# Prompt attention: the causal mask of the diagonal block, added to the decay rows by GpSimd and taken back by VectorE, in place of bf16 products on TensorE

## The reference

```
s = jnp.einsum('bqhd,bkhd->bhqk', q_blk, k) * (FOX_HD ** -0.5)
s = s + (cq_blk[..., :, None] - ckT[..., None, :])      # cumulated log forget values of query and key
s = jnp.where(kpos[None, :] <= qpos[:, None], s, -jnp.inf)
p = jax.nn.softmax(s, axis=-1)
o = jnp.einsum('bhqk,bkhd->bqhd', p, v)
```

## Time and profile before

| | us |
|---|---|
| median of 3 runs | 1659.86 |
| lowest and highest run | 1656.78, 1660.15 |
| the profiled execution | 1657.8 |
| its span | 1656.2 |

### The profile page before, as it was taken

The page is one execution under the profiler, slowest core; times in us unless marked ns, Lnnn a source line. Parts: engine busy times, 40 slices in busy tenths (PEclk is TensorE's granted clock), DMA queues, the critical chain, the costliest instruction groups (busy, mean ns, idle before and its releaser), DMA issues. The chain is left out here.

```text
span 1656.2 us, 25654 instructions
## 1 busy us (share of the span) xinstructions
PE 1545.4 (93%) x9795; PEld 1401.9 (85%) x9795; DVE 848.9 (51%) x1434; ACT 663.0 (40%) x1117; POOL 241.2 (15%) x297
## 2 busy tenths in 40 slices
PE   7999999999999998999999999999996699999980
PEld 6999899889988887888999999999785588888860
DVE  4433463454035555532232223324657799999985
ACT  5422141212145555521121112113112588888866
POOL 1000111013001211140000000000000345243320
PEclk9999999999999999999999999999997799999995
DMA  6111132124221112073262114103533799999746
GB/s 188 42 39 39 55 117 67 39 67 146 69 81 45 72 46 81 20 236 110 84 198 63 39 39 146 44 34 117 178 115 123 264 260 269 333 301 283 188 64 235
DMA packets 154226, 204.35 MB, mean 123 GB/s; under 512 B 14723, under 2 KB 121235, under 8 KB 154104
## 3 DMA queue, kind: packets, MB, share of 16 engines
q1 hardware_dynamic: 135224, 140.82, 27.2%
q0 software_dynamic: 18880, 61.89, 13.4%
HBM read 152.34 MB, written 50.34 MB: 122 GB/s over the span
## 5 line engine op out<-in xcount | busy, mean ns | idle before, releaser
L380 PE MATMUL ps<-xh,slab_hi 128*128 128x384 f32 (+1 forms) x504 | 170.5, 338 | 1.4 <-DVE slab_lo L733 1.4
L380 PE MATMUL ps<-xh,slab_lo 128*128 128x384 f32 (+1 forms) x504 | 165.2, 328 | 0.0
L380 PE MATMUL ps<-xl,slab_hi 128*128 128x384 f32 (+1 forms) x504 | 164.8, 327 | 0.0
L1906 PE MATMUL ps<-xh,slab_lo 128*128 128x384 f32 (+1 forms) x384 | 125.2, 326 | 0.0
L1906 PE MATMUL ps<-xh,slab_hi 128*128 128x384 f32 (+1 forms) x384 | 125.1, 326 | 0.0
L1906 PE MATMUL ps<-xl,slab_hi 128*128 128x384 f32 (+1 forms) x384 | 125.1, 326 | 0.0
L2122 DVE TENSOR_TENSOR gt_sg<-ps,gt_sg 128x384 f32<-128x384 f32 (+1 forms) x48 | 25.7, 536 | 187.3 <-PE ps L1906 187.2
L380 PEld LDWEIGHTS ps<-xh,slab_hi 128*128 128x128 f32 x504 | 95.1, 189 | 11.5 <-issue 9.7
L2898 PE MATMUL ps<-mo_hi_gu,mo_xh 128*128 128x512 f32 x256 | 100.3, 397 | 0.9 <-ACT mo_xh L3001 0.7
L2062 ACT ACTIVATE gt_sg<-ps 128x384 f32<-128x384 f32 (+1 forms) x48 | 22.8, 474 | 191.9 <-PE ps L1906 191.8
L2898 PE MATMUL ps<-mo_hi_gu,mo_xl 128*128 128x512 f32 x256 | 99.4, 393 | 0.0
(11 more groups left out here) (501 smaller groups left out, 4123.3 us busy)
## 6 DMA issues: line engine op xcount, KB each, us to landing
slab_raw<-in_w_in SPq DMA_DIRECT2D x60, 512.0 KB, 4.2
mo_raw_g<-in_w_e_gate SPq DMA_DIRECT2D x16, 1024.0 KB
mo_raw_u<-in_w_e_up SPq DMA_DIRECT2D x16, 1024.0 KB
mo_raw_d<-in_w_e_down SPq DMA_DIRECT2D x16, 1024.0 KB
gt_oh<-oT_hi SPq DMA_DIRECT2D x3, 2176.0 KB, 9.3
gt_ol<-oT_lo SPq DMA_DIRECT2D x3, 2176.0 KB, 14.0
slab_raw<-in_w_branch SPq DMA_DIRECT2D x24, 256.0 KB, 4.7
x_dram<-slab_raw SPq DMA_DIRECT2D x9, 512.0 KB, 5.1
```

Source lines behind the costliest of these rows:

```text
L380: mm = eng.matmul(out, w[:, b, k, :], x[:, k, t0:t0 + tn], start=(k == 0 and j == 0), stop=(k == KC - 1 and j == 2), skip_group_check=True)
L1906: last = eng.matmul(out, w[:, s % 2, c, wk, :], x[:, k, t0:t0 + tn], start=(k == 0 and i == 0), stop=(k == ks[-1] and i == 2))
```

## The change

The bf16 products go, and with them `mpos`, `ident16` and TensorE's wait for them. A buffer `plain` of three places is new. For block Q, GpSimd's `mask_block(Q)` first copies the decay rows of the block's own 128 keys, for both heads, to `plain`, then adds the mask tile `mf` to them in place. It does this three blocks ahead: for Q = 0, 1, 2 before the loop, and for Q + 3 at the head of its loop step Q. It waits for the rows' load where a pair begins, and for `lowest` of block Q - 2, head 0, before it uses a place of `plain` again. VectorE, before `lowest(Q, 0)`, copies the plain values of block Q - 1 back (not where a pair begins, since those rows aren't read again before they are loaded anew), waits for its own copy, and waits for GpSimd's count, so that the mask of block Q is there.

```diff
-    RW, RH = 2, 4
+    RW, RH, RC = 2, 4, 3
...
-        mpos, ident16 = sb("mpos", [128, 128], BF16), sb("ident16", [128, 128], BF16)
-        mf = sb("mf", [128, 128])
+        mf, plain = sb("mf", [128, 128]), sb("plain", [128, RC, 2, 128])
...
+        def own_block(Q):
+            p, qt = divmod(Q, 8)
+            return cb[:, 2 * (p % 2):2 * (p % 2) + 2, 128 * qt:128 * qt + 128]
...
+            def mask_block(Q):
+                if Q % 8 == 0:
+                    eng.wait_ge(c_in[Q // 8 % 2], 32 * (Q // 16 + 1))
+                if Q >= RC:
+                    eng.wait_ge(s_out, out_no[Q - RC + 1, 0, 0] + 1)
+                ch(eng.tensor_copy(plain[:, Q % RC, :, :], own_block(Q)))
+                ch(eng.tensor_tensor(own_block(Q), own_block(Q), mf[:, :].unsqueeze(1).broadcast_to([128, 2, 128]), ALU.add))
...
-            ch(eng.tensor_copy(mpos[:, :], mf[:, :]))
-            ch(eng.tensor_copy(ident16[:, :], sh.ident[:, :]))
             rows(0)
             rows(1)
+            for Q in range(RC):
+                mask_block(Q)
...
             for Q in range(NQ):
                 p, qt = divmod(Q, 8)
+                if Q + RC < NQ:
+                    mask_block(Q + RC)
                 eng.wait_ge(oT_lo, Q + 1)
...
-                    diag = k0 + n == 128 * (qt + 1)
...
-                                            start=(j == 0), stop=(j == 2 and not diag), skip_group_check=True)
-                    if diag:
-                        for h in range(2):
-                            mm = eng.matmul(sh.ps[:, s_bank(Q, h, c), n - 128:n], ident16[:, :], mpos[:, :], start=False,
-                                            stop=True, skip_group_check=True)
+                                            start=(j == 0), stop=(j == 2), skip_group_check=True)
...
-            eng.wait_ge(pool_s, 4)
             scores(0)
...
+                if h == 0:
+                    if Q % 8:
+                        ch(eng.tensor_copy(own_block(Q - 1), plain[:, (Q - 1) % RC, :, :]))
+                    eng.wait_ge(pool_s, 2 + 2 * (Q + 1))
                 for c in range(n_chunk(Q)):
```

## The result

| | us |
|---|---|
| before, median of 8 runs beside the changed kernel | 1660.01 (1656.78 to 1664.94) |
| after, median of 8 runs | 1666.58 (1664.71 to 1669.67) |
| ratio after to before, 95% interval | 1.0043 (1.0031 to 1.0055) |
| the profiled execution of after, its span | 1667.2, 1665.6 |

The account below looks back on a forecast made before the run. TensorE was taken to set the pace, with VectorE delays counting only where chains through ScalarE end in TensorE's waits. Products -1.5, copies +3.0, collisions +3.2 gave +4.7 us: 1662.5 profiled, 1664.5 as median forecast, range 1657.5 to 1669.5.

Parts of the forecast that it names:

- The gain of the products: TensorE's 64 bf16 mask products go: 0.07 us per block, kept in 22 of 32 blocks, 1.5 us gained (0 to 4.4).
- the nine places: Blocks Q = 3, 5, 7, 11, 13, 15, 19, 21, 28, where VectorE's delay reaches TensorE's wait through ScalarE; no product gain kept.
- block 24's: Block where TensorE waits for a long tail of VectorE, so the removed products were forecast to gain nothing.
- The uncovered copies: VectorE's copies before `lowest` without idle time to cover them: nine blocks by 0.33 us, 3.0 us lost (1.5 to 4.1).
- Rival (b): VectorE's copies never reach TensorE, which keeps all its gain: 2.2 to 6.4 us, 1653.5 to 1657.7 us; chance 0.12.
- The collisions: GpSimd's copy and add hold VectorE's tails and normalisations on the uncovered chains: sum 3.4, taken as 3.2 us (0 to 5.6).
- the row, 0.04 us lost of 0.18 in common: Trace before: VectorE `tensor_tensor` of 128x16 took 0.21 us, not 0.17, beside GpSimd's 128x128 select; read as a small hold.
- rival (e): Every VectorE-GpSimd overlap is paid in full and the add takes 0.78 us: +7.1 us, 1667.0 us; chance 0.07.
- Rival (a): No collisions, GpSimd's copy and add run freely beside VectorE: +1.5 us, 1661.4 us; chance 0.36.
- Rival (c): GpSimd's copy and add slip 20 us, so VectorE waits for late masks: 1671 us or more; chance 0.04.
- Rival (d): The change doesn't do what it says: products stay or other bf16 rows replace them; 1660 us, chance 0.01.

Follow-up runs that it names:

- experiment 2: Changed kernel with VectorE's copies only, bringing back zeros written once, GpSimd's copy and add left out; measured +1.7 us (+0.2 to +3.2) against the kernel before.
- experiment 3: Changed kernel with GpSimd's copy and add kept and VectorE's 28 copies left out; measured +2.0 us (+0.5 to +3.5) against the kernel before.
- experiment 4: Changed kernel with VectorE's copy moved from the head of `lowest(Q, 0)` to behind `out_tail` of the step before; measured +2.8 us (+1.3 to +4.5) against the kernel before.
- Experiment 8: The changed kernel measured again, nothing altered, on the same chip as the other follow-up kernels; +5.6 us (+3.5 to +8.0) against the kernel before, span 1662.5 us.

## Why the prediction was right

**The gain of the products** (forecast 1.5 us from 22 blocks at 0.07). TensorE in order of time behind the scores of block 9, the step of the earlier trace rows, after:

```profile
539.08 0.44 PE L1216 MATMUL ps<-xh,slab_hi 128*128 128x384 f32 x1
539.36 0.34 PE L1216 MATMUL ps<-xl,slab_hi 128*128 128x384 f32 x1
```

0.28 us, the very number of the earlier trace rows. Without a mask, the steps outside the nine places and block 24's are shorter by 1.43 us together, 0.07 each; the nine add 0.26, which the prediction put at nothing. What decided was to price the products by the step that stays when they are gone. By their records, 64 of 0.22 us, one would have expected 14 us.

**The uncovered copies** (forecast 9 x 0.33 = 3.0). Measured 2.9, in the nine places and nowhere else. Reading each chain backwards, from TensorE's wait through ScalarE's queue to a VectorE without idle time before `lowest`, found all nine. Rival (b), that the copies never arrive, falls by experiment 2.

**The collisions** (forecast 3.2, from a sum of 3.4, rounded down without a reason; experiment 3: 3.5). The sum is right by luck: its terms are not, and two errors cancel. The prediction gave 0.2 us to the places Q = 5, 13 and 21; those lost 0.47 to 0.53. In the other direction it charged 0.5 at Q = 11, 15 and 19, which lost 0.26 to 0.28. Two of its inputs were off. It took GpSimd's add at 0.60 us; it takes 0.73. (The 0.7 us that it names as an estimate was near, though not the plain eighth of the 4497 ns beside it, which is 0.56.) And it placed the pair too early. GpSimd's stores begin 0.30 us behind the end of `out_tail` in the kernel before, but in nearly all steps 0.54 behind it in every kernel here that has the pair or the memsets in GpSimd's loop. At Q = 13, before and after:

```profile
558.59 0.29 DVE L1507 TENSOR_TENSOR fx_ol<-ps,fx_oh 128x128 fp32r<-128x128 f32 x1 [0.46 <-ACT fx_oh L1403]
559.18 0.54 POOL L99 DMA_DIRECT2D oT_hi<-fx_oh  x1 [5.76 <-DVE fx_ol L1507]
```

```profile
560.52 0.29 DVE L1518 TENSOR_TENSOR fx_ol<-ps,fx_oh 128x128 fp32r<-128x128 f32 x1 [0.47 <-ACT fx_oh L1410]
561.35 0.56 POOL L99 DMA_DIRECT2D oT_hi<-fx_oh  x1 [4.37 <-DVE fx_ol L1518]
```

Why GpSimd starts later isn't shown. So the add begins 0.10 us ahead of the key tail and not 0.36, and they have 0.63 us in common where the prediction had 0.24. At Q = 11 the same delay makes GpSimd's copy, forecast to precede the weight tail, start level with it, and there the prediction overlooked that VectorE holds GpSimd as well; the copy waits out the whole tail:

```profile
549.22 1.23 DVE L1030 TENSOR_TENSOR slab_lo<-slab_raw,slab_hi 128x1024 fp32r<-128x1024 f32 x1 [1.66 <-ACT slab_hi L1023]
549.22 1.47 POOL L1136 COPY fx_plain<-fx_cb 128x256 f32<-128x256 f32 x1
...
551.08 0.70 DVE L1513 TENSOR_SCALAR fx_P<-fx_P,fx_rinv 128x384 f32<-128x384 f32 x1
```

After that the add meets only the second normalisation and costs it 0.28 us (0.70 instead of 0.42). Q = 3 is of the same kind, but there the copy began 0.07 us ahead of the tail (experiment 3): it lost 0.50. Q = 7, with 0.43, and Q = 28, with 0.28, came out near their forecast.

The Trainium skill ("SBUF — State Buffer", section "SBUF: two separate sides") states this rule: the shared pair of ports is locked from the start of an instruction to its end, against VectorE operations with two SBUF inputs only by a GpSimd operation that reads SBUF, and against those in a two-port mode by any. The traces agree at each point: 0.91 us for 0.42 beside the add, a weight tail at its 1.23 beside two memsets, 0.69 for the minima whose second operand is in PSUM. The prediction took the row, 0.04 us lost of 0.18 in common, for a partial hold, set it above the rule and gave rival (e) only 0.07. Read beside the runs, this row is a full hold. The key tail of Q = 13 lost 0.49 us of 0.63 in common, the weight tail of experiment 4 0.20 of 0.34: 0.14 less than the common time, as in the row. The normalisations lost 0.20 less (0.28 of 0.49 at Q = 15). Rival (e) was nearer in the add's duration and in the full hold. Its 5.6 us of holds were still too many against 3.5, since a full lock also delays GpSimd and takes later overlaps away.

**The sum.** Forecast -1.5 + 3.0 + 3.2 = +4.7; traces 4.9; measured +7.1 and +5.6 by the ratios. The 1664.5 forecast stands 2.1 us under the median. Experiment 8 shows that two executions of this kernel with the same attention can lie 3.1 us apart by the clock and the experts' stage; that this is the cause of the 2.1 is not shown. Rival (a) falls by experiment 3. Rival (c) asked for a late pair. The profile names GpSimd once as what VectorE waited for (0.4 us, at 662.54, minima of block 26), but the instruction named makes the mask of a later block, and before VectorE stood there for the scores; no late mask is seen. Rival (d) falls by the counts of the page.

## What to carry to other kernels

Taking small products from the engine that bounds a kernel gains the difference of the steps with and without them, not their recorded time (here 0.07 us per block, not 0.45), and that must pay for every instruction put ahead of a chain that ends in that engine's wait. GpSimd is no free helper while VectorE works from SBUF to SBUF: start its reads when VectorE reads PSUM, by waiting for the event that ends the SBUF work. Here that one changed wait took back nearly all of the holds, and moving the copy into VectorE's idle time took back most of the copies' cost (2.9 to 0.6 us in the nine steps).

## What the runs showed of the hardware that I had not expected

- The hold goes both ways: GpSimd's copy of 128x256 took 0.40 us alone and 1.47 beside a weight tail of 1.23, its add 0.73 alone and up to 1.82.
- What VectorE loses to a reading GpSimd instruction follows the time that the two records have in common: 0.14 us less than it for a `tensor_tensor`, about 0.20 less for a `tensor_scalar`.
- In the kernels with two more instructions in GpSimd's loop, GpSimd's first store began 0.54 us behind the instruction that it waits for, not 0.30. That moved its pair by a quarter of a microsecond against VectorE's work; why isn't shown.
- A copy of VectorE that began 0.14 us before GpSimd's copy left both at their own duration (0.29 and 0.40 us), although the records overlap by 0.15. That is about the 0.14 us that costs nothing above; which record starts early or ends late isn't shown.
- A memset on GpSimd doesn't hold a `tensor_tensor` of VectorE (1.23 us as alone), but is itself held by a `tensor_scalar` (0.77 us instead of 0.33).
- One half-clock stretch of TensorE costs 1.2 to 1.6 us, and two executions of the same program had them at different times and in different number. The experts' stage differed by another 1.9 us at the full clock. Differences of 2 us between two profiles of this kernel say nothing until they have been traced to their place, step by step.
